# Causal attention: the later queries' 256 weight columns are scaled by ScalarE instead of VectorE

## The reference

```python
# q block i of 128 queries: i = 0, 1; 256 keys
s = q @ k.T * scale + bias            # (heads, 128, 256)
s = where(key_pos <= q_pos, s, -inf)
p = softmax(s, axis=-1)               # exp(s - max) / sum
o = p @ v
```

## Time and profile before

| | |
|---|---|
| median of 3 runs | 1420.13 us (1419.01 to 1421.72) |
| the profiled execution | 1420.94 us, of which the span is 1419.1 us |
| instructions in the span | 19398 |
| TensorE matmuls busy | 1368.3 us (96%) |
| VectorE busy | 972.2 us (69%) |
| ScalarE busy | 675.8 us (48%) |
| GpSimd busy | 72.8 us (5%) |
| causal attention, fox | about 640 to 680 us of the span |
| causal attention, odd | about 1150 to 1210 us of the span |

### The profile page before, as it was taken

The page is one execution under the profiler, slowest core; times in us unless marked ns, Lnnn a source line. Parts: engine busy times, 40 slices in busy tenths (PEclk is TensorE's granted clock), DMA queues, the critical chain, the costliest instruction groups (busy, mean ns, idle before and its releaser), DMA issues.

```text
span 1419.1 us, 19398 instructions
## 1 busy us (share of the span) xinstructions
PE 1368.3 (96%) x7690; PEld 1163.8 (82%) x7690; DVE 972.2 (69%) x1319; ACT 675.8 (48%) x1052; POOL 72.8 (5%) x111
## 2 busy tenths in 40 slices
PE   7999999999999999998999999999999978999997
PEld 5988988888878888887788888888888865888886
DVE  5686776666687767558467676776676677576674
ACT  5476454443655434455554444444444456444432
POOL 1400000000000000003000000000000143000000
PEclk9999999999999999999899999999999999999999
DMA  8333556555546555454246555465554443465550
GB/s 299 124 129 120 178 171 208 186 191 187 163 150 201 191 189 182 157 175 142 89 149 208 180 192 189 163 205 197 181 181 153 161 131 98 138 207 203 179 185 38
DMA packets 66938, 240.26 MB, mean 169 GB/s; under 512 B 7919, under 2 KB 8312, under 8 KB 66848
## 3 DMA queue, kind: packets, MB, share of 16 engines
q1 hardware_dynamic: 64624, 233.14, 49.5%
q0 software_dynamic: 1936, 5.78, 1.5%
q10 hardware_dynamic: 288, 0.11, 0.0%
HBM read 237.84 MB, written 1.09 MB: 168 GB/s over the span
## 4 chain that ended last, share of the span: by engine, by line
PE 74%; issue 14%; DVE 6%; ACT 3%; DMA 1%; POOL 0%; DVEq 0%; POOLq 0%; ACTq 0%
PE pp L452 73%; DVE wlo L1582 2%; PE pp L461 2%; ACT whi L1161 1%; DVE hx L1590 1%; ACT pbuf L1308 1%; DVE fa L1582 1%; DVE pbuf L1586 0%; ACT xn L1200 0%; ACT hx L1162 0%; DMA gns<-gains 0%; DVE fa L1579 0%; DVE xn L1582 0%; DVE X L1590 0%; DVE fa L1590 0%
## 5 line engine op out<-in xcount | busy, mean ns | idle before, releaser
L452 PE MATMUL pp<-hx,whi 128*128 128x512 f32 (+1 forms) x2400 | 729.4, 365 | 8.4 <-DVE hx L1590 3.0
L1582 DVE TENSOR_TENSOR wlo<-raw,whi 128x1024 fp32r<-128x1024 f32 (+1 forms) x443 | 523.0, 1221 | 156.8 <-ACT whi L1161 156.6
L452 PE MATMUL pp<-hx,wlo 128*128 128x256 f32 x2032 | 569.7, 280 | 0.0
L452 PEld LDWEIGHTS pp<-hx,whi 128*128 128x128 f32 x2400 | 427.5, 189 | 91.7 <-issue 10.2
L1161 ACT ACTIVATE whi<-raw 128x1024 fp32r<-128x1024 f32 (+1 forms) x443 | 441.5, 1045 | 108.2 <-PE pp L452 105.7
L452 PEld LDWEIGHTS pp<-hx,wlo 128*128 128x128 f32 x2032 | 384.8, 189 | 2.1
L452 PE MATMUL pp<-whi,ra 128*128 128x512 f32 x1144 | 372.0, 396 | 0.0
L452 PEld LDWEIGHTS pp<-whi,ra 128*128 128x128 f32 x1144 | 215.9, 189 | 50.5 <-issue 1.2
L452 PE MATMUL pp<-wlo,ra 128*128 128x512 f32 x572 | 225.6, 394 | 0.0
L1662 DVE TENSOR_REDUCE fa<-pp 128x512 f32<-128x1024 f32 x104 | 127.0, 1221 | 82.7 <-PE pp L452 82.7
L1161 ACT ACTIVATE ra<-fa 128x512 fp32r<-128x512 f32 x63 | 39.8, 632 | 230.9 <-DVE fa L1590 230.9
(11 more groups left out here) (164 smaller groups left out, 783.3 us busy)
## 6 DMA issues: line engine op xcount, KB each, us to landing
raw<-w_chunks SPq DMA_DIRECT2D x439, 512.0 KB, 5.0
fa<-t_rows POOLq DMA_DIRECT2D x16, 128.0 KB, 3.3
X<-x_in SPq DMA_DIRECT2D x2, 512.0 KB, 5.5
fa<-g_fin POOLq DMA_DIRECT2D x2, 512.0 KB, 3.8
fa<-f_rows POOLq DMA_DIRECT2D x8, 128.0 KB, 3.2
out_dram<-X SPq DMA_DIRECT2D x2, 512.0 KB, 2.7
cst<-consts POOLq DMA_DIRECT2D x1, 840.0 KB, 6.5
fa<-g_qk POOLq DMA_DIRECT2D x1, 320.0 KB, 6.3
```

The source lines that it names most:

```text
L452: return pe.matmul(o, lhs, rhs, start=first, stop=last, skip_group_check=True)
L1582: return dve.tensor_tensor(o, a, b, op)
```

## The change

ScalarE gets, behind the four exponentials and `evict` of a pair and ahead of `one_more(p, 0)`, two more instructions in both causal attentions: for each head it waits for that head's reciprocal (`s_rcp`) and multiplies the 256 columns of the later queries in place by it, counting the new semaphore `s_sha`. VectorE scales only the 128 columns of the earlier queries there, and counts `s_shr` behind them. TensorE's `turn_weights` waits for both. The attentions of the first block stay as they were. The causal attentions have 24 heads in 12 pairs.

```diff
@@ -650,6 +650,8 @@
                     pe.wait_ge(s_shr, h0 + h + 1)
+                    if causal:
+                        pe.wait_ge(s_sha, h0 - 16 + h + 1)
                     if h >= len(tbk):
                         pe.wait_ge(s_ptc, h0 + h + 1 - len(tbk))
@@ -1309,6 +1311,11 @@
                         y.then_inc(s_ex)
                     evict((name, p, 0))
+                    for h in (2 * p, 2 * p + 1) if causal and p < pairs else ():
+                        o = weights_slot(name, h)[:, 128:384]
+                        rs = head_stats(h0 + h)[2]
+                        act.wait_ge(s_rcp, h0 + h + 1)
+                        copy(o, o, scale=rs[:, 1:2]).then_inc(s_sha)
                     one_more(p, 0)
@@ -1781,7 +1788,7 @@
                         dve.wait_ge(s_ex, hc + 1)
                         dve.reciprocal(rs, sm).then_inc(s_rcp)
                         dve.wait_ge(s_rcp, hc + 1)
-                        for t in range(2):
+                        for t in range(1 if causal else 2):
                             sl = slice(off[t], off[t] + kl[t])
                             y = ts(o[:, sl], o[:, sl], rs[:, t:t + 1], None, ALU.mult, None)
                         y.then_inc(s_shr)
```

More of the change, by code:

```diff
@@ L225, in program @@
         s_diag, s_spread, s_rb, s_c0 = [sem(n) for n in ("s_diag", "s_spread", "s_rb", "s_c0")]
-        s_sc, s_smax, s_negm, s_ex, s_rcp, s_shr, s_ptn, s_ptc, s_pv, s_ohs, s_ols = [
-            sem(n) for n in ("s_sc", "s_smax", "s_negm", "s_ex", "s_rcp", "s_shr", "s_ptn", "s_ptc", "s_pv",
+        s_sc, s_smax, s_negm, s_ex, s_rcp, s_shr, s_sha, s_ptn, s_ptc, s_pv, s_ohs, s_ols = [
+            sem(n) for n in ("s_sc", "s_smax", "s_negm", "s_ex", "s_rcp", "s_shr", "s_sha", "s_ptn", "s_ptc", "s_pv",
                              "s_ohs", "s_ols")]
```

## The result

The changed kernel takes 1437.61 us (median of 4 runs, 1434.83 to 1438.67), the kernel before in the same comparison 1420.93 (1419.01 to 1421.99). The ratio is 1.011, 95% interval 1.0095 to 1.0126: slower, by 16.7 us. The forecast was 1431.1 with a range to 1436.5, so the direction held and the size did not.

The account below looks back on a forecast made before the run. The prediction took the kernel as TensorE-bound, with loops of latencies in both causal attentions. Loop terms of 9.6 us plus 1.4 for the clock made 11.0, added to the median 1420.13: 1431.1 us, range 1424.5 to 1436.5.

Parts of the forecast that it names:

- What bounds the kernel, and the loop: Both causal attentions: a loop of latencies through TensorE, VectorE and ScalarE, with TensorE waiting mostly for ScalarE's copy to `ptb`.
- Two ScalarE scalings at 0.40 us each in the queue: Each pair, between exponentials and `ptb` copy: 0.80 us added, 9.6 us of ScalarE time over 12 pairs.
- plain rounds: Odd rounds 4, 5 and 7: reciprocal ready once the first new scaling is done, price 0.8 us each, 2.4 together.
- The wait for the reciprocals: ScalarE's second scaling waits for VectorE: copy 2.75 us later in fox round 1, 2.05 in odd round 2.
- The give-back: VectorE's delay in the next round shrinks, returning 1.15 us after fox round 1 and 0.45 after odd round 2.
- The sum of the loop: Both causal attentions: scalings and waits less what VectorE's delays give back, 9.6 us slower.
- the list of signs: Expected in the profile after: among others, fox longer by about 3.4 us (5 with the clock), odd by 6.2.
- The clock: Fox round 1: TensorE at its lower clock after a 5.8 us wait, price between 0 and 2.05 us, taken as 1.4.
- rival (c): Clock falls in more places, two more stretches in odd rounds 2 to 4 and fox's rest: 1435.9 us, chance 0.16.
- (a): Rival: VectorE's relief, 3.1 us, wins and the new work fits ScalarE's idle time: 1417.0 us, chance 0.06.
- (b): Rival: the reciprocal wait costs nothing, only the scalings in 10 rounds less relief, 4.9 us: 1425.0 us, chance 0.14.
- (d): Rival: gain and loss cancel within 0.2%, with VectorE's relief and half of the scalings hidden; chance 0.04.

Follow-up runs that it names:

- fox-only run: The changed kernel with 38 idle TensorE matmuls in fox round 1 alone: 1432.17 us, ratio to before 1.0089.
- reciprocals-first run: The changed kernel with VectorE taking both reciprocals of a pair ahead of both its 128-column scalings: 1435.6 us, ratio to before 1.0092.
- relief run: The changed kernel with nobody scaling the later queries' 256 columns and nobody waiting for it: 1421.62 us, ratio to before 0.9998.
- wait-only run: The changed kernel with ScalarE waiting for both reciprocals of the pair, the 256-column scaling left out everywhere: 1430.34 us, ratio to before 1.0057.

## Why the prediction was off

**What bounds the kernel, and the loop:** right. The copy to `ptb` was what ended TensorE's wait in before, and it still is, later. Putting the same work behind that copy takes the loss away.

**Two ScalarE scalings at 0.40 us each in the queue:** right. The profile after has

```profile
L1164 ACT ACTIVATE pbuf<-pbuf,st 128x256 f32<-128x256 f32 x24 | 11.2, 500 | 3.8 <-DVE st L1789 3.8
```

with a mean of 500 ns where the eviction had shown 476, and 0.80 us for a pair in the plain rounds. By the Trainium skill ("ScalarE: Activation LUTs", What ACT_TABLE_LOAD costs) the estimate is 0.49 us for one, overlapping the next by 0.09. The trace agrees: 0.49 to 0.51 for one, 0.80 in the queue for two.

**The wait for the reciprocals:** right in kind, and where the numbers meet, partly by luck. Fox round 1: copy at 652.61 where I had worked out 652.5 (the second reciprocal's end, 651.1 there, comes to 651.0 by its own terms). But the round itself began 0.84 us later than in before, since the two scalings of round 0 push back ScalarE's two splits (exponentials 0 to 1 took 0.80 us more), and the sum has no term for round 0. Within the round the copy came 2.0 us later, not 2.75, so round 1 cost a net 0.8 and not 1.6, and round 0 the other 0.8. Odd round 2: exponentials to turning 1.56 longer, of which I had 1.55. There VectorE's scaling beside GpSimd (0.97 us) made the second reciprocal late, which my working didn't have at that length; in the fox-only run the same round was 0.85 longer. In odd round 5, which I had as plain (0.8), it was 1.35: VectorE's first scaling took 1.38 us beside GpSimd and held the second reciprocal back. The reciprocals-first run removes that piece.

**The give-back:** 1.2 in fox and 0.28 in odd where I had 1.15 and 0.45, and 0.52 of head start in odd round 0 where I had 0.5. It is there in the rounds of after, but alone it is no measurable gain.

**The sum of the loop:** 9.6 forecast, 10.3 measured (fox 3.6 where the terms add up to 3.6, odd 6.7 where they add up to 6.0; the 3.4 and 6.2 in the list of signs are not the sums of these terms). The agreement in fox is of the total, not of its rounds. The miss of the total doesn't lie here.

**The clock:** the step that failed. I took one stretch, fox round 1, at 1.4 us, and held the odd rounds to be as in before. Fox was 1.9. Odd rounds 1, 3 and 5 ran at or near half clock (means of 0.50 to 0.55), which cost 6.5 us against 3.6 in before, 2.9 more: 4.8 in the attentions where the sum had 1.4. Of the 1.8 us between the stages, for which the sum had nothing, 1.5 stand at low clock too. That is rival (c) in kind, 1435.9, to which I gave 0.16, but its number is near by luck as well: it has 4.1 us for two more stretches in odd rounds 2 to 4, where one new stretch (round 5, 1.8) and two longer ones (1.1) were measured, and nothing between the stages. I treated the clock as something that happens where a wait exceeds before's longest (4.9 us). The trace of before spoke against such a bound. In it odd round 3 had a mean granted clock of 0.64 behind a wait of 2.4 us:

```profile
1176.81 0.52 PE L461 MATMUL pp<-cst,pbuf 128*128 128x128 f32 x3 [2.38 <-ACT ptb L1161]
```

Fox round 1 stayed at 1.00 behind 3.0. With seven waits of the loop lengthened by 0.8 us and more, more low-clock stretches were the likely case and belonged into the forecast. The Trainium skill ("TensorE: Matmul & The Clock Gate", The HAM clock gate) says that TensorE without work falls to half its clock. The trace agrees: with idle matmuls in the gaps the same stretches ran at 1.00.

**The rivals:** (a), relief wins, is out by the relief run, which gains nothing. (b), the wait costs nothing, is out by the wait-only run. (d) is out: the ratio is 1.011.

What stays open: where the low clock falls in a given execution. Executions of one kernel differ by 2 to 8 us (the relief run from 1415.58 to 1423.80), and a stretch of 10.2 us at low clock behind fox in before's profile, and in after's, is 6.8 us in others, such as that of after with idle matmuls. From inside it, in before and in that run:

```profile
686.50:696.40 9.90, 9.90 (x24) 6.55 (x25) 1.46 (x3) 3.82 (x5) 0.00 (x0) 0.50 0.31 105
...
689.60:696.20 6.60, 6.60 (x17) 4.32 (x18) 0.60 (x2) 1.88 (x2) 0.00 (x0) 0.50 0.46 155
```

Where each comes from wasn't tested. Each kernel was profiled once, so a difference of 1 or 2 us between two profiles may be such a stretch and not the change; the loop's intervals at full clock repeat to about 0.02 us in the plain rounds and to some 0.7 where VectorE and GpSimd meet.

## What to carry to other kernels

In a software pipeline an engine with idle time is not free at every place in its queue: ask what is queued behind the new instruction and who waits for that, and put moved work behind the step that the bounding engine waits for. A new wait costs what is ahead of it on the other engine. Even at its best place the moved work gained nothing here that could be measured, as the relief run would have it. And when TensorE's waits grow at many places, price the clock at all of them, not at the longest; the number is the same matmul stretch at either level.

## What was not expected of the hardware

Idle matmuls in TensorE's gaps pay for themselves: 141 of them made after 9.5 us faster (7.0 of 10.0 in the attentions, by the profiles), and 80 made before 4 us faster (0.9973, 0.9962 to 0.9984). Those that outlasted the awaited copy cost their excess, 0.5 to 1.5 us in a round. A wait of 2.55 us was followed by a mean granted clock of 0.71 in one kernel, one of 3.03 by 1.00 in another.
